# The last merge of a two-block transformer kernel with channels as rows: one branch's gate by seven block products, the other branch in token halves

## The reference, cut to what matters

```
gate_logits = u @ w_in[:, 3104:5152]                 # u: normed rows, 512 x 1024
y_a = rwkv7_branch(...)   # a recurrence over the tokens, group norm, then  rows @ w_out_a (512 x 1024)
y_b = mla_branch(...)     # attention, then                                  rows @ w_out_b (512 x 1024)
gates = sigmoid(gate_logits + b_gate)                # g_a: first 1024 columns, g_b: last 1024
mixed = g_a * y_a + g_b * y_b
h = h + rmsnorm(mixed @ w_o, g_post)
```

## Time and profile before

| | |
|---|---|
| median of 3 runs | 1371.72 us |
| lowest, highest | 1369.55, 1372.11 us |
| the profiled execution | 1376.24 us, its span 1374.8 us |
| mean granted TensorE clock | 0.993 |
| TensorE matmul busy | 1325.9 us, 96% of the span |
| VectorE, ScalarE, GpSimd busy | 572.7, 338.6, 477.2 us |
| the changed stage (merge and recurrence) | from 1061 to 1317 us of the span |
| the last product and the end | from 1317 to 1375 us |

### The profile page before, as it was taken

The page is one execution under the profiler, slowest core; times in us unless marked ns, Lnnn a source line. Parts: engine busy times, 40 slices in busy tenths (PEclk is TensorE's granted clock), DMA queues, the critical chain, the costliest instruction groups (busy, mean ns, idle before and its releaser), DMA issues. The chain is left out here.

```text
span 1374.8 us, 24524 instructions
## 1 busy us (share of the span) xinstructions
PE 1325.9 (96%) x10316; PEld 808.6 (59%) x10316; DVE 572.7 (42%) x1389; ACT 338.6 (25%) x788; POOL 477.2 (35%) x586
## 2 busy tenths in 40 slices
PE   8999998999999999999999979999999899999997
PEld 7876445788887474444444335467677445665543
DVE  5366126841415263322111153462388571343315
ACT  3225126631010110111111033462312211322221
POOL 8667503774643901222222302063241011111061
PEclk9999999999999999999999999999999999999999
DMA  8291315021311687999999942011311332200221
GB/s 280 75 361 63 92 61 189 1 66 61 123 61 61 216 304 255 374 381 378 379 381 382 400 172 77 8 62 62 119 65 57 98 108 77 80 2 18 90 95 61
DMA packets 100913, 213.07 MB, mean 155 GB/s; under 512 B 14709, under 2 KB 23760, under 8 KB 100672
## 3 DMA queue, kind: packets, MB, share of 16 engines
q1 hardware_dynamic: 88272, 173.49, 35.3%
q0 software_dynamic: 12528, 37.97, 8.1%
HBM read 190.98 MB, written 19.42 MB: 153 GB/s over the span
## 5 line engine op out<-in xcount | busy, mean ns | idle before, releaser
L1602 POOL TENSOR_TENSOR AR<-Wt,AR 128x512 f32<-128x512 f32 x68 | 88.6, 1323 | 98.7 <-PE pb L1803 92.8
L3958 PE MATMUL pb<-Wt,HT 128*128 128x512 f32 x256 | 117.8, 602 | 1.8 <-DVE AR L4049 1.8
L2504 PE MATMUL pb<-AR 128*64 128x512 f32 x256 | 85.0, 595 | 0.7 <-issue 0.7
L2713 POOL DMA_DIRECT2D ys<-AR x28 | 15.1, 544 | 182.0 <-ACT AR L2677 182.0
L3958 PEld LDWEIGHTS pb<-Wt,HT 128*128 128x128 f32 x256 | 46.4, 190 | 53.6 <-issue 49.2
L1803 PE MATMUL pb<-AR 128*128 128x256 f32 x320 | 73.2, 380 | 2.5 <-POOL AR L1602 1.3
L2504 PE MATMUL pb<-Wt,AR 128*64 128x512 f32 x192 | 70.8, 595 | 0.0
L1803 PEld LDWEIGHTS pb<-AR 128*128 128x128 f32 x320 | 60.2, 190 | 12.1 <-POOL AR L1602 2.2
L1602 POOL TENSOR_TENSOR AR<-Wt 128x512 f32<-128x512 f32 x34 | 44.2, 1320 | 63.1 <-DMA Wt<-in_w_in_dram 31.1
L1803 PE MATMUL pb<-HT,Wt 128*128 128x256 f32 x288 | 65.0, 380 | 0.0
L832 POOL TENSOR_SCALAR X<-X,SM 128x384 f32<-128x384 f32 (+2 forms) x64 | 39.0, 622 | 74.2 <-DVE SM L786 74.2
(11 more groups left out here) (590 smaller groups left out, 2608.6 us busy)
## 6 DMA issues: line engine op xcount, KB each, us to landing
Wt<-in_w_in_dram SPq DMA_DIRECT2D x17, 2048.0 KB, 8.0
AR<-in_w_gate_dram SPq DMA_DIRECT2D x8, 2048.0 KB, 19.7
AR<-in_w_up_dram SPq DMA_DIRECT2D x8, 2048.0 KB, 19.0
AR<-in_w_down_dram SPq DMA_DIRECT2D x8, 2048.0 KB, 18.4
Wt<-in_w_gate_dram SPq DMA_DIRECT2D x6, 2048.0 KB, 21.1
Wt<-in_w_down_dram SPq DMA_DIRECT2D x6, 2048.0 KB, 15.2
Wt<-in_w_up_dram SPq DMA_DIRECT2D x6, 2048.0 KB, 21.3
ys<-AR POOLq DMA_DIRECT2D x2, 3072.0 KB, 25.6
```

The costliest lines, as they stand in the source:

```text
L1602: r = gt.tensor_tensor(out[:, k:k + s, :], a[:, k:k + s, :], b[:, k:k + s, :], op)
L2504: r = mm(s[o:o + 64, :], XT[b % 2][:, k, 0:64], W.ap((n, b))[:, k, :], start=k == 0, stop=k == 7)
L2713: gt.dma_start(ys_dram[r0:r0 + 64, 512 * c:512 * c + 512], y[64 * c:64 * c + 64, 0:512]).then_inc(s_yst[b % 2], 16)
L3958: r = mm(s, HT[:, k, t * 128:(t + 1) * 128], W.ap(("gate2", c, br))[:, k, :], start=k == 0, stop=k == 7)
```

## The change

- Branch b's gate is made with channels as rows by two `Quarters` units (`gate7b`, one for each half of the channels), woven in as `product` steps: 14 products of 8 matmuls 128x256. They use two token sums kept from the units before and two new ones (`late_sums`); all sums are formed by `branch_sums_po` on GpSimd, ahead of `chunks_po`. The bias comes as a column (`bcol`) and is added by ScalarE in the sigmoid.
- Branch b's up is 8 products [128 channels x 512 tokens] of 4 matmuls, from one load `up2b` of 2 MB in place of two of 1 MB.
- Branch a's gate and up are made in halves of 256 tokens and pairs of channel tiles (`halves_pe`): matmuls of 256 columns, twice as many. A step (yield) is two such matmuls, half the work of a step before. The gates of half 0 and the first of half 1 come ahead of the wait for chunk 1; `oA` is turned for t = 0 and 1 together; ups of half 0, one gate, turn 2, two gates, then two steps of the last product, turn 3 and the ups of half 1.
- The mixed rows need no turn; the 8 mixed turns go. The first step of the last product and the ScalarE copies of it stand in `dense_*` now; GpSimd's first two weight sums for it come before the wait for the mixed rows.
- The key products of `alT` and `rT` are one matmul of 64 columns (`rTalT`, a strided view) in place of two of 32.
- The store and reload of the block products follows the loads of both gate weights and of `up2b` on SyncE's queue.

```diff
@@ class Quarters
+                self.left_at = use.get("left_at", (1, 2, 3, 4))
             def p5_pe(self):
-                pe.wait_ge(self.left_sem, 1)
+                pe.wait_ge(self.left_sem, self.left_at[0])
...
-        sgr = [mp.take(512) for _ in range(2)]
-        yb1 = mp.take(512)
+        sgr = [mp.take(2, 256) for _ in range(2)]
+        yb1 = mp.take(2, 256)
...
-        mx = Place(AR, ARN, tail_at).take(4, 1024)
+        sgr += [obp.take(2, 256) for _ in range(2)] + [p6s2]
+        mxT = Place(AR, ARN, tail_at).take(8, 512)
...
+            use = dict(sems=(*quarter_sems, s_left2), tokens=HT, lefts=(*token_sums[0:2], *late_sums),
+                       left_at=(1, 2, 5, 6), rights=(*weight_sums[0:2], W.ap(("gate2", c, 1))[:, 4:8, 0:256]),
+                       copies=(dst[:, 0:2, hi], dst[:, 2:4, hi], dst[:, 2:4, lo]), late=None,
+                       weights=lambda tag: (tag, W.ap(tag)))
+            gate7b.append(Quarters(("gate2", c, 1), 7 + len(merge7) + c, use, dst, False, (units + gate7b)[-1]))
...
+        def branch_sums_po():
+            a11, a21, a12 = HT[:, 0:4, 0:256], HT[:, 0:4, 256:512], HT[:, 4:8, 0:256]
+            s2, (s3, s4) = token_sums[1], late_sums
+            for c, u in enumerate(gate7b):
+                t1, t2, t4 = u.rights
+                po.wait_ge(*W.loaded(u.name))
+                po.wait_ge(*u.before.part(1))
+                tiles_po(t1, u.b12, u.b11, ALU.subtract, s_right4)
+                po.wait_ge(*u.before.part(2))
+                po.wait_ge(*u.right(1))
+                tiles_po(t2, u.b22, t1, ALU.subtract, s_right4)
+                if c == 0:
+                    po.wait_ge(s_app, 4)
+                    tiles_po(s4, a12, s2, ALU.subtract, s_left2)
+                    tiles_po(s3, a11, a21, ALU.subtract, s_left2)
+                tiles_po(u.b12, u.b22, u.b12, ALU.subtract, s_right4)
+                po.wait_ge(*P.filled(u.key("x")))
+                po.wait_ge(*u.right(2))
+                tiles_po(t4, u.b21, t2, ALU.subtract, s_right4)
...
                     for i in range(4):
-                        for j, x in enumerate((alT, rT)):
-                            for hp in range(2):
-                                k0, c0 = 128 * t + 32 * i, 64 * n + 32 * j
-                                r = mm(s[hp][32 * i:32 * i + 32, c0:c0 + 32], ch(kaT, n, hp, k0, k0 + 32),
-                                       ch(x, n, hp, k0, k0 + 32), start=True, stop=True)
+                        for hp in range(2):
+                            k0 = 128 * t + 32 * i
+                            r = mm(s[hp][32 * i:32 * i + 32, 64 * n:64 * n + 64].rearrange("p (x q) -> p x q", q=32),
+                                   ch(kaT, n, hp, k0, k0 + 32), rTalT[64 * hp:64 * hp + 64, :, n, k0:k0 + 32],
+                                   start=True, stop=True)
...
+        def halves_pe(key, name, nk, w, c0, x, hf):
+            pe.wait_ge(*W.loaded(name))
+            s = P.take(pe, "O", key)
+            for j in range(2):
+                for k in range(nk):
+                    r = mm(s[:, 256 * j:256 * j + 256], w[:, k, c0 + 128 * j:c0 + 128 * j + 128],
+                           x[:, k, 256 * hf:256 * hf + 256], start=j == k == 0, stop=k == nk - 1, skip_group_check=True)
+                    if j and k == nk - 1:
+                        r.then_inc(P.full(key), 1)
+                        W.last(name, key)
+                    if k % 2:
+                        yield 1
+
+        def gate_pe(hf, p):
+            name = ("gate2", p // 2, 0)
+            yield from halves_pe(("g2", hf, p), name, 8, W.ap(name), 256 * (p % 2), HT, hf)
...
+        def dense_pe(ended):
...
+            for f in (b0.p1_pe, b0.p5_pe, b0.p2_pe, b0.p6_pe, b0.p3_pe, b0.p7_pe, b1.p1_pe, b0.p4_pe, b1.p5_pe, b1.p2_pe,
+                      b1.p6_pe):
+                yield from product(f)
+            for g, f in enumerate((b1.p3_pe, b1.p7_pe, b1.p4_pe)):
+                yield from branch_up_pe(g)
+                yield from product(f)
+            yield from branch_up_pe(3)
+            yield from gate_pe(0, 0)
+            for g in range(4, 8):
+                yield from branch_up_pe(g)
+            for p in (1, 2, 3):
+                yield from gate_pe(0, p)
+            yield from gate_pe(1, 0)
+            while 1 not in ended:
+                yield 1
+            for t in range(2):
+                yield from rows_turn_pe(t)
+            for t in range(2):
+                pe.wait_ge(*P.drained(("oAt", t)))
+            for p in pairs:
+                yield from up_pe(0, p)
+            yield from gate_pe(1, 1)
+            while 2 not in ended:
+                yield 1
+            yield from rows_turn_pe(2)
+            for p in (2, 3):
+                yield from gate_pe(1, p)
+            while "values" not in ended:
+                yield 1
+            for _ in range(2):
+                next(final_steps[0])
+                yield 1
+            while 3 not in ended:
+                yield 1
+            yield from rows_turn_pe(3)
+            for t in (2, 3):
+                pe.wait_ge(*P.drained(("oAt", t)))
+            for p in pairs:
+                yield from up_pe(1, p)
...
+        def sigmoid_ac(hf, p):
+            key, z = ("g2", hf, p), sig_of[hf][p]
+            ac.wait_ge(*P.filled(key))
...
+            for j in range(2):
+                r = st.activation(z[:, j, :], P.ap(key)[:, 256 * j:256 * j + 256], ACT.Sigmoid,
+                                  bias=bcol[:, 2 * p + j:2 * p + j + 1])
...
-            po.wait_ge(*P.filled(("oAt", 3)))
-            fin7.right_po(1)
-            for c in range(2):
-                po.wait_ge(*P.drained(("g2", 0, c, 3)))
-                for t in ALLT:
-                    po.wait_ge(*P.drained(("mxt", c, t)))
+            po.wait_ge(s_mix2, 8)
             fin7.left_po(mxT, 1)
-            fin7.right_po(2)
             fin7.left_po(mxT, 2)
             fin7.left_po(mxT, 3)
+            po.wait_ge(*P.filled(("oAt", 3)))
             fin7.right_po(3)
...
             for c in range(2):
                 load(("gate2", c, 1), wcols(w2, 3104 + 1024 + 512 * c, 512))
-                load(("up2", c, 1), wcols(a["w_out_b_2"], 512 * c, 512, 512))
-                if c == 0:
-                    inverse_sy()
+            load("up2b", a["w_out_b_2"].rearrange("(k p) n -> p k n", p=128))
+            inverse_sy()
             for c in range(2):
                 load(("gate2", c, 0), wcols(w2, 3104 + 512 * c, 512))
             load("up2a", a["w_out_a_2"].rearrange("(k p) n -> p k n", p=128))
```

More of the change, by code:

```diff
@@ L3952, in chunks_ve @@
             yield 1
[L3954 to L3961 removed]
+        pairs = range(4)
+        sig_of = {0: {p: sgr[p] for p in pairs}, 1: {p: sgr[(4 + p) % 5] for p in pairs}}
@@ L3962, in gate_pe, with branch_up_pe @@
+        sig_n = {}
+        def branch_up_pe(g):
+            pe.wait_ge(*W.loaded("up2b"))
+            pe.wait_ge(s_ob, 1)
+            s = P.take(pe, "O", ("u2b", g))
+            for k in range(4):
+                r = mm(s, W.ap("up2b")[:, k, 128 * g:128 * g + 128], oBT[:, k, :], start=k == 0, stop=k == 3)
+                if k == 3:
+                    r.then_inc(P.full(("u2b", g)), 1)
+                    W.last("up2b", ("u2b", g))
                 if k % 2:
                     yield 1
-        def up_pe(br, c, t, lT, w, name):
+        def halves_pe(key, name, nk, w, c0, x, hf):
@@ new lines, in dense_ac @@
+            for g in range(6, 8):
+                branch_sigmoid_ac(g)
+            yield from pause(4)
+            sigmoid_ac(0, 0)
+            yield from pause(8)
+            for p in (1, 2, 3):
+                yield from pause(8)
+                sigmoid_ac(0, p)
+            yield from pause(8)
+            sigmoid_ac(1, 0)
+            while 1 not in ended:
+                yield 1
+            for t in range(2):
+                yield from rows_turn_ac(t)
+            yield from pause(4 * 4)
@@ new lines, in dense_ac @@
+            yield from pause(8)
+            sigmoid_ac(1, 1)
+            while 2 not in ended:
+                yield 1
+            yield from rows_turn_ac(2)
+            for p in (2, 3):
+                yield from pause(8)
+                sigmoid_ac(1, p)
+            while "values" not in ended:
+                yield 1
+            for i in range(2):
+                yield 1
+                fin7.first_ac(i, None)
+            while 3 not in ended:
+                yield 1
+            yield from rows_turn_ac(3)
```

298 lines of the change are left out of this document (154 added, 144 removed).

## The result

The changed kernel takes 1393.7 us (median; 1385.8 to 1397.6), the kernel before 1371.9: the measured ratio is 1.0145, with a 95% interval of 1.0118 to 1.0173. By the ratio that is 20 us slower (the two medians are 21.8 us apart), four times the 4.7 us forecast, and 1393.7 lies outside the range given. Run again on another chip it stood at 1.0143 (1.0126 to 1.0160). The profiled execution took 1394.3 us, its span is 1393.0.

The account below looks back on a forecast made before the run. TensorE, busy 96% of the span, was taken as the bound. With 19.0 us added and 14.3 removed, the forecast was 4.7 us slower, a median of 1371.7 + 4.7 = 1376.4 us, range 1367.5 to 1382.5.

Parts of the forecast that it names:

- (1): Branch b's gate: fourteen products of 3.52 us replace eight tiles of 6.92 us, a gain of 6.1 us.
- (2): Turns after the last chunk: the mixed turns and 8 later transposes go, a gain of 4.6 us.
- (3): Paired key products in the four chunks: 0.46 us saved in each, 1.8 us in all; bounds 0 and 2.6.
- (4): TensorE's wait for VectorE's bias addition behind the inverse's first rows goes with L4049, a gain of 1.8 us.
- (5): Ahead of the last product, TensorE idles for the last w_o load: 8.2 us added; bounds 7.3 and 10.5.
- (6): Behind the w_o load's wait, TensorE's clock is low for the next products: 2.0 us added; bounds 0 and 3.4.
- (7): Ahead of the block products, GpSimd's weight sums slow VectorE beside them: 2.6 us added; bounds 0 and 5.0.
- (8): First seven-product unit: TensorE waits for VectorE's c22 behind the inverse's rows, 2.6 us added; bounds 1.0 and 5.0.
- (9): Behind chunk 3, gate (1, 0)'s sigmoid stands among ScalarE's copies: TensorE waits 2.6 us; bounds 0.5 and 3.6.
- (10): Chunks 1 to 3: dense steps of half the work cover awaited copies less, 1.0 us added; bounds 0 and 8.
- Rival D: GpSimd's four sum instructions each block VectorE for their whole length: 5.0 us instead of 2.6; 1378.8 us; chance 0.09.
- Rival C: Only thick steps had hidden the chunks' recurrence, so thin cover costs its upper bound: +11.7, 1383.4 us; chance 0.08.

Follow-up runs that it names:

- the control: The changed kernel itself with no edit, run again on the chip of its variants: ratio 1.0143 to the kernel before.
- the run with the three edits at the end: Changed kernel with the late w_o half awaited where read, chunk 3's norm later, turns of chunks 0 and 1 ahead of gate (1,0): ratio 1.0005.
- the turns first: Changed kernel with the turns of chunks 0 and 1 ahead of gate (1,0) instead of behind it: ratio 1.0117.
- the run with thick steps: Changed kernel with gate and up matmuls in token halves four at a time between chunk steps instead of two, pauses halved: ratio 1.0236.
- unpaired products: Changed kernel with the key products as two matmuls of 32 columns again instead of one of 64: ratio 1.0140.
- the seven repairs: Changed kernel: load awaited where read, norm and GpSimd's sums later, ScalarE's copy and turns earlier, both units' c22, c12 and c21 moved forward among inverse rows: ratio 0.9950.

## Why the prediction was wrong

The signs that it named came true: the long wait ahead of the first L1673 with the slower clock behind it, the block products at 1072.13, the products 3.5 us apart. What it removes was about right: 14.3 us with 3.3 of old waits in it, so 11.0 of work, against 10.1 in the ledger. What it adds was put at 19.0 us and is 33.6 (22.4 and the 3.3 of old waits, and 7.9 of clock). Step by step:

- **(1)** Seven products: right. Uninterrupted they follow each other 3.5 us apart, as foretold.
- **(2)** Mixed turns: no L838 run is left at the end but chunk 3's four. The copies behind turns still cost 0.49 and 0.74 us.
- **(3)** Paired products: 0.54 us a chunk in the trace, 2.2 us in four; not resolved in the time. The 0.46 of the prediction set a busy length (0.86, with the drain) against a time from start to start (1.32); the two busy lengths, 1.40 and 0.86, give the 0.54.
- **(4)** The wait for the bias went with its line.
- **(5), (6)** The load: 7.80 us against 8.2, and 1.5 us of clock (3.0 in the control) against 2.0. Together 10.2 foretold, 10.6 measured by taking the wait away. What this wait costs by itself was the best part of the prediction.
- **(7)** GpSimd beside VectorE: the mechanism is right, the size was not. I counted three operations of VectorE held up by 0.9 us each, 2.6 us; its chain took 13.3 instead of 8.5 us, 4.8 more, and TensorE waited 3.83 + 0.39. The higher value came from the Trainium skill ("SBUF — State Buffer", section "Who interferes with whom"), by which the loser is blocked for the whole instruction. The rows agree with it: a copy of 16 columns takes 1.06 us beside a sum of GpSimd's and 0.17 alone, and it ends at 1063.61, just behind GpSimd's operations (1063.57).
- **(8)** `c22` behind the inverse: 2.70 us against 2.6 as a wait, which is partly luck. From the end of the block products `c22` took 23.6 us instead of 20.3, and TensorE's work up to there 21.1 instead of 18.1, since it was itself slowed by the clock. Where the clock did not slow it, in the run with the three edits at the end, the wait is 3.47. And I priced one wait, where it is the first of a row of them.
- **(9)** The sigmoid among the copies: 1.52 + 0.73 = 2.25 us against 2.6; removing it gave 3.6, give or take 3.3.
- **(10)** Thin cover, 1.0 us. The issue gaps of the chunks are 6.05 us against 2.24, 3.8 more. But they vary from run to run (4.9 in the control, 3.0 with the turns first, 3.4 in the kernel before with paired products), and the run with thick steps has 5.4. So it isn't shown that thin steps lengthen them, and their cause stays open.
- **What the list lacked**: `up_ve(0, 0)` behind chunk 3's norm, 3.52 us. Among the nothings I wrote of the ups of half 1 behind the last chunk; the ups of half 0 I took to be free, without asking what stands ahead of their reader on VectorE. That was the question that the first part of the prediction said must be asked.
- **The step that failed most is (6)**, as a rule: I charged the clock to the longest wait alone. The granted clock fell behind the waits of 3.83, 2.70 and 3.52 us too, 6.4 us more than the 1.5 behind the load. Of the rows that I read, one showed the fall behind 5.48 us of idle time (0.56), another none behind 1.78 us (7.13 us for what takes 7.03 elsewhere). Between the two I had no row, and took waits of 2.6 us to be free of it.

The parts of the missing 14.6 us, in the profiled execution: 5.9 of clock beyond the 2.0; 3.5 for the norm; 2.8 of issue gaps beyond (10); 1.6 for (7); 1.4 in short waits of 0.16 to 0.74; less 0.7 on (5), (8) and (9). Of these the clock and the issue gaps differ between two executions of the same kernel: in the control the clock cost some 7 us beyond the 2.0, and the gaps 1.6 beyond (10). Rival D had about the right size for (7). Rival C came nearest in time, but by luck: it blamed thin steps, and thick ones made the kernel slower. No case had the sum.

## What to carry to other kernels

When an order is rewritten, go through each engine's program at each hand-over and ask what stands ahead of the reader, also for the work that you don't think of as changed; and price each new wait of TensorE with the slower clock that may follow it: here waits of 2.4 to 7.9 us cost 0 to 3.1 us on top. Where several engines' programs are woven, a repair that leaves the time as it was proves nothing about its cause: the same loss may come up at the next product. Put the repairs together before you call a cost nothing.

## What the runs showed of the hardware

The same wait does not always have the same price. Behind the wait of 2.70 us for `c22` the sixteen records took 5.09 us in the changed kernel, 3.69 in its control and 6.74 with unpaired products (2.71 us there). Behind 3.52 us at the ups the clock fell in both executions of the changed kernel (8.86 and 8.85 in place of 7.07). Behind 3.82 us ahead of the block products, the sixteen records that follow these took 6.59 us in the control, but 3.72 in the run with the three edits at the end: there the clock stood at 0.59 from 1070 to 1073, while the small products ran (2.85 us in place of 2.34), and was back at 1.00 for the large ones.

Short gaps can do it too. In the seven repairs the granted clock was 0.53 behind the wait of 2.38 us for the masks, where sixteen records took 2.04 us in place of 1.16, and 0.50 behind an issue gap of 1.85 us, where twelve took 7.06 in place of 5.42. In the kernel before, it stayed at 1.00 behind gaps of 1.97 and 1.78 us. The Trainium skill ("TensorE: Matmul & The Clock Gate", section "Why this matters for your kernels") warns of idle gaps between bursts; here gaps of half the length and less of the one that I had read it for were enough, and shorter than those that it warns of.

The issue gaps, mostly 0.5 to 2.4 us, come in streams of hundreds of small matmuls. The one inside the block products is in every run (1.6 to 2.4 us; ahead of the last of 256 records in the changed kernel, behind 143 in the kernel before). Those in the chunks come at the same few places in many runs, but are absent or elsewhere in others, with lengths that vary. Nothing that the profile names ends them.
